# Prompts' residual rows stored to the output in the output projection, expert rows added onto them by scattering transfers

## The reference

```python
expert_id = g_sel[:, None] * EXPERTS_PER_GROUP + top_i          # two experts of each token
gate = jnp.sum(one_hot(expert_id, N_EXPERTS) * (g_w * top_p)[..., None], axis=1)
hid = silu(t @ w_gate[e]) * (t @ w_up[e]) * gate[:, e]
out = sum over e of hid @ w_down[e]
xp = xp + mp[5] * moe(modulate(xp, ...))                        # prompts: one gate row mp[5] for all tokens
xs = xs + ms[5] * moe(modulate(xs, ...))                        # samples: a gate row per token
```

## Time and profile before

| | us |
|---|---|
| median of 3 runs | 837.73 (836.27 to 840.06) |
| profiled execution, its own time | 836.97 |
| span of the profile | 835.2 |
| PE busy | 750.3 (90%) |
| DVE busy | 413.1 (49%) |
| ACT busy | 205.8 (25%) |
| POOL busy | 168.5 (20%) |

### The profile page before, as it was taken

The page is one execution under the profiler, slowest core; times in us unless marked ns, Lnnn a source line. Parts: engine busy times, 40 slices in busy tenths (PEclk is TensorE's granted clock), DMA queues, the critical chain, the costliest instruction groups (busy, mean ns, idle before and its releaser), DMA issues.

```text
span 835.2 us, 11189 instructions
## 1 busy us (share of the span) xinstructions
PE 750.3 (90%) x4235; PEld 463.8 (56%) x4235; DVE 413.1 (49%) x925; ACT 205.8 (25%) x417; POOL 168.5 (20%) x192
## 2 busy tenths in 40 slices
PE   4999989999989978999999899887999999998760
PEld 2444454588756545887886354554555555554330
DVE  4124499998798988101133123683443333333326
ACT  4012333223476664002002011122111111111100
POOL 2030030320000000443202002353223333233010
PEclk9999999999999998999999979896999999999995
DMA  8951041533236343233022902147999999999928
GB/s 350 402 179 63 2 131 39 202 114 106 101 144 260 112 189 119 110 133 127 20 101 111 407 20 101 53 177 269 412 429 423 425 424 426 423 424 422 413 124 308
DMA packets 25903, 183.65 MB, mean 220 GB/s; under 512 B 6460, under 2 KB 6884, under 8 KB 14456
## 3 DMA queue, kind: packets, MB, share of 16 engines
q1 hardware_dynamic: 15800, 161.06, 47.7%
q0 software_dynamic: 9456, 19.72, 7.1%
q10 hardware_dynamic: 592, 2.13, 0.6%
HBM read 178.59 MB, written 14.12 MB: 231 GB/s over the span
## 4 chain that ended last, share of the span: by engine, by line
PE 76%; DMA 11%; DVE 5%; ACT 4%; issue 2%; SPq 1%; POOL 1%; DVEq 0%; POOLq 0%; ACTq 0%
PE psum L735 24%; PE psum L1229 12%; PE psum L704 9%; PE psum L1243 6%; DMA arena<-in_experts 5%; PE psum L668 3%; PE psum L1130 3%; DMA arena<-in_b_router 2%; PE psum L614 2%; PE psum L1222 2%; DMA ring<-in_stream 2%; ACT arena L1588 2%; DVE arena L2576 1%; PE psum L1089 1%; PE psum L923 1%
## 5 line engine op out<-in xcount | busy, mean ns | idle before, releaser
L735 PE MATMUL psum<-hT,ring 128*128 128x260 f32 x640 | 145.8, 389 | 8.1 <-DMA ring<-in_stream 8.1
L735 PEld LDWEIGHTS psum<-hT,ring 128*128 128x128 f32 x640 | 122.5, 193 | 30.7 <-DMA ring<-in_stream 9.0
L1588 ACT ACTIVATE arena<-psum 128x512 f32<-128x512 f32 (+10 forms) x130 | 69.3, 563 | 242.6 <-PE psum L735 79.9
L704 PE MATMUL psum<-ring,hT 128*128 128x512 f32 (+1 forms) x256 | 98.0, 537 | 3.4 <-DVE arena L2298 3.4
L704 PEld LDWEIGHTS psum<-ring,hT 128*128 128x128 f32 x256 | 49.0, 197 | 50.8 <-issue 37.6
L1229 PE MATMUL psum<-ring,arena 128*64 128x256 f32 x608 | 70.5, 385 | 3.6 <-DMA ring<-in_experts 3.6
L1243 PE MATMUL psum<-arena 128*64 128x512 f32 x280 | 67.8, 604 | 3.3 <-issue 2.0
L1527 POOL DMA_INDIRECT expert_rows<-arena,router x35 | 35.4, 1010 | 154.7 <-DVE arena L2536 154.7
L1229 PEld LDWEIGHTS psum<-ring,arena 128*64 128x64 f32 x608 | 43.8, 139 | 34.2 <-issue 8.9
L735 PE MATMUL psum<-arena,ring 128*128 128x260 f32 x256 | 58.6, 392 | 0.0
L2535 DVE SCALAR_TENSOR_TENSOR arena<-psum,router,arena 128x512 f32<-128x512 f32 x35 | 26.3, 751 | 64.4 <-PE psum L1243 64.4
(11 more groups left out here) (381 smaller groups left out, 953.9 us busy)
## 6 DMA issues: line engine op xcount, KB each, us to landing
ring<-in_stream SPq DMA_DIRECT2D x21, 2048.0 KB, 8.5
ring<-in_experts SPq DMA_DIRECT2D x16, 2048.0 KB
arena<-in_experts SPq DMA_DIRECT2D x32, 1024.0 KB
arena<-in_experts SPq DMA_DIRECT2D x11, 2048.0 KB
hT<-in_experts SPq DMA_DIRECT2D x5, 2048.0 KB
ring<-expert_rows SPq DMA_DIRECT2D x8, 512.0 KB, 6.9
ring<-in_stream SPq DMA_DIRECT2D x2, 1280.0 KB, 5.6
arena<-in_x_prompt SPq DMA_DIRECT2D x4, 512.0 KB, 5.3
```

What stands on the lines that cost most here:

```text
L704: mm = pe.matmul(psum[:, b, 0:width], hT[:, k, t * P:(t + 1) * P], w[:, k, :], start=(k == 0), stop=(k == KD - 1))
L735: mm = pe.matmul(psum[:, b0 + s, 0:HALF], w[:, k, f * P:(f + 1) * P], rhs[:, k, s * HALF:(s + 1) * HALF], start=(first and k == 0), stop=( ...
L1588: ins = act.activation(out, in_, func, scale=scale)
```

## The change

- ACT stores each prompt tile of `x2` to `y_p` right behind that tile's `t2_store` (four transfers of 512 KB), counted by `sums_begun`.
- POOL stores zeros to the first 8 rows of `expert_rows`, which become the samples' sums (`zeros_stored`). The zeros come from `zero_rows`, which DVE sets beforehand. ACT waits for this store before it writes `gate_table`, which shares the space.
- `scatter` becomes two transfers per block, both with `compute_op=ALU.add`: one adds onto `y_p` by `token_tab` (bound: the prompts' rows), one onto the samples' sums by `dest_tab` (bound: 16 half rows). Each skips the other's tokens.
- A token's two picks go to the same row now, so the scatters must not overlap: `scatter(b)` waits first until both transfers of block b-1 have landed. Block 0 waits for `sums_begun` and `zeros_stored`.
- `y_stored` counts 32 per block instead of 16, and so do the waits on it.
- `dest_tab` is made in `is_sample` from `token_tab`; `sent_to` makes only `token_tab`.
- At the end SP reads the samples' sums back (32 KB), DVE multiplies them by the gate and adds them to `x2`, and SP stores `y_s`. The ten reads of picks, the ten additions on DVE and the four stores of `y_p` there are gone.
- The overflow blocks are changed likewise, with a wait behind each pair of transfers.

```diff
@@ sync
-                lone_wait(sp, over_stored, i * 32 + 32, over_passed)
+                lone_wait(sp, over_stored, i * 64 + 64, over_passed)
...
-            by_token = picks.rearrange("(c t h) n -> c t (h n)", c=2, h=2)
             for i in range(2):
-                sp.wait_ge(y_stored[i], 16 * ((N_MAIN + 1 - i) // 2))
-            for _, n, t in LAST_ORDER:
-                for c in range(2):
-                    sp.dma_start(picked[c][t][0:n], by_token[c, t * P:t * P + n, :]).then_inc(picked_in[t], 16)
-            for i, (_, n, t) in enumerate(LAST_ORDER):
-                sp.wait_ge(y_ready, i + 1)
-                dst = io["y_p"][t * P:(t + 1) * P, :] if t < NT else io["y_s"]
-                sp.dma_start(dst, x2[0:n, t, :]).then_inc(y_outs, 16)
-            sp.wait_ge(y_outs, 16 * T5)
+                sp.wait_ge(y_stored[i], 32 * ((N_MAIN + 1 - i) // 2))
+            sp.dma_start(sample_sums, io["expert_rows"][0:NS, :]).then_inc(sample_sums_in, 16)
+            sp.wait_ge(y_s_ready, 1)
+            sp.dma_start(io["y_s"], x2[0:NS, NT, :]).then_inc(y_outs, 16)
+            sp.wait_ge(y_outs, 16)
@@ gpsimd
             second_rstd(0)
+            pool.dma_start(io["expert_rows"][0:NS, :].rearrange("r (q n) -> (r q) n", q=4), zero_rows)\
+                .then_inc(zeros_stored, 16)
             second_rstd(1)
...
             def scatter(b):
                 label = BLOCKS[b][1]
-                pool.indirect_dma_start(picks, bass.IndirectOffsetOnAxis(dest_tab[:, label:label + 1], 0),
-                                        y_rows[:, b % 2, :], None, bounds_check=4 * TOK - 1, oob_is_err=False)\
-                    .then_inc(y_stored[b % 2], 16)
+                if b == 0:
+                    pool.wait_ge(sums_begun, 16 * NT)
+                    pool.wait_ge(zeros_stored, 16)
+                else:
+                    pool.wait_ge(y_stored[1 - b % 2], 32 * ((b - 1) // 2 + 1))
+                for sums, tab, rows in ((sums_p, token_tab, 2 * SEQ), (sums_s, dest_tab, 2 * NS)):
+                    pool.indirect_dma_start(sums, bass.IndirectOffsetOnAxis(tab[:, label:label + 1], 0),
+                                            y_rows[:, b % 2, :], None, bounds_check=rows - 1, oob_is_err=False,
+                                            compute_op=ALU.add).then_inc(y_stored[b % 2], 16)
@@ scalar
                 act.dma_start(io["t2_rows"][t * P:t * P + n, :], t2[i % 2][0:n, :]).then_inc(t2_stored[i % 2], 16)
+                if t < NT:
+                    act.dma_start(io["y_p"][t * P:(t + 1) * P, :], x2[:, t, :]).then_inc(sums_begun, 16)
...
             x_out(0, xT_out)
+            act.wait_ge(zeros_stored, 16)
             evac("gate_sums", ...)
@@ vector
+            lane.mark(dve.memset(zero_rows, 0.0))
...
-            banks.drained(sent_to(token_tab[:, 0:N_MAIN], dest_tab[:, 0:N_MAIN], psum[:, 4, 0:N_MAIN], sent), "tables")
+            sent_to(token_tab[:, 0:N_MAIN], psum[:, 4, 0:N_MAIN], sent).then_inc(tables_ready, 1)
+            dve.wait_ge(tables_ready, 1)
+            banks.drained(dve.tensor_copy(sent, token_tab[:, 0:N_MAIN]), "tables")
...
             def is_sample(tokens, n):
-                lane.then(dve.tensor_copy(tokens, token_tab[:, o]))
+                lane.mark(dve.tensor_scalar(prompt_skip[:, 0:n], tokens, 2.0 * SEQ, SKIP, ALU.is_lt, ALU.mult))
                 lane.then(dve.scalar_tensor_tensor(sample_gate[:, o], tokens, 2.0 * SEQ, gate_tab[:, o], ALU.is_ge, ALU.mult))
+                lane.mark(dve.scalar_tensor_tensor(dest_tab[:, o], tokens, 2.0 * SEQ, prompt_skip[:, 0:n],
+                                                   ALU.subtract, ALU.add))
...
                     if b >= 3:
-                        dve.wait_ge(y_stored[1 - p], 16 * ((b - 1) // 2))
+                        dve.wait_ge(y_stored[1 - p], 32 * ((b - 1) // 2))
...
-            for _, rows, t in LAST_ORDER:
-                dve.wait_ge(picked_in[t], 32)
-                for c in range(2):
-                    x, a = x2[0:rows, t, :], picked[c][t][0:rows]
-                    if t == NT:
-                        lane.then(dve.tensor_tensor(a, a, gate2_s[0:NS], ALU.mult))
-                    ins = dve.tensor_tensor(x, x, a, ALU.add)
-                    lane.then(ins) if c == 0 else ins.then_inc(y_ready, 1)
+            dve.wait_ge(sample_sums_in, 16)
+            lane.then(dve.tensor_tensor(sample_sums, sample_sums, gate2_s[0:NS], ALU.mult))
+            dve.tensor_tensor(x2[0:NS, NT, :], x2[0:NS, NT, :], sample_sums, ALU.add).then_inc(y_s_ready, 1)
```

More of the change, by code:

```diff
@@ L414, in decoder_step @@
         sent = at(6656, N_MAIN)
+        prompt_skip = at(6656 + 192, N_MAIN)
         r = sb("router", [P, 630])
@@ L469, in decoder_step @@
         over_sent = at(6656 + 2 * SB, N_OVER)
-        picked = [[ring[:, 1 + c, t * D:(t + 1) * D] for t in range(NT)]
-                  + [hT.rearrange("p k n -> p (k n)")[:, c * D:(c + 1) * D]] for c in range(2)]
+        sample_sums = x_rows[0:NS, 0:2, :].rearrange("p b n -> p (b n)")
+        zero_rows = at(32768, 256)[0:4 * NS]
         bank_full = [sem(f"bank_full{b}") for b in range(8)]
@@ L533, in decoder_step @@
         over_scaled, over_gated = sem("over_scaled"), sem("over_gated")
-        picked_in = [sem(f"picked_in{t}") for t in range(T5)]
-        y_ready = sem("y_ready")
+        sums_begun, zeros_stored, sample_sums_in, y_s_ready = (
+            sem(n) for n in ("sums_begun", "zeros_stored", "sample_sums_in", "y_s_ready"))
         ws_masked = sem("ws_masked")
@@ L551, in decoder_step @@
         last_use = {}
-        LAST_ORDER = [("S", NS, NT), (0, P, 0), (1, P, 1), (2, P, 2), (3, P, 3)]
         ROUTE = [(P, 0), (NS, NT), (P, 1), (P, 2), (P, 3)]
@@ L557, in decoder_step @@
         half_rows = io["t2_rows"].rearrange("r (h n) -> (r h) n", h=2)
-        picks = io["expert_rows"].rearrange("r (h n) -> (r h) n", h=2)[0:4 * TOK, :]
+        sums_p = io["y_p"].rearrange("r (h n) -> (r h) n", h=2)
+        sums_s = io["expert_rows"].rearrange("r (h n) -> (r h) n", h=2)[0:2 * NS, :]
         def lone_wait(engine, semaphore, value, passed):
@@ L1547, in pool_pair @@
                 for n in range(2):
-                    pool.wait_ge(y_stored[n], 16 * ((N_MAIN + 1 - n) // 2))
+                    pool.wait_ge(y_stored[n], 32 * ((N_MAIN + 1 - n) // 2))
                 for j in range(2):
@@ L1567, in pool_pair @@
                     lone_wait(pool, over_y_out, i * 2 + j + 1, over_passed)
[L1568 to L1571, removed]
+                    for sums, tab, rows in ((sums_p, next_token, 2 * SEQ), (sums_s, next_dest, 2 * NS)):
+                        pool.indirect_dma_start(sums, bass.IndirectOffsetOnAxis(tab[:, j:j + 1], 0),
+                                                y_rows[:, j, :], None, bounds_check=rows - 1, oob_is_err=False,
+                                                compute_op=ALU.add).then_inc(over_stored, 16)
+                    lone_wait(pool, over_stored, i * 64 + 32 * j + 32, over_passed)
                 pool.sem_inc(over_go, 1)
@@ L2430, in _, with sent_to @@
                 psum[0:NE, 2, 0:P].rearrange("p (h n) -> p h n", h=2), 2, 2)), "picks")
-            def sent_to(token, dest, V, tmp):
+            def sent_to(token, V, tmp):
                 lane.then(dve.tensor_scalar(tmp, V, C("second_at"), -2.0 * TOK, ALU.is_ge, ALU.mult))
-                ins = dve.scalar_tensor_tensor(token, V, C("half_at"), tmp, ALU.add, ALU.add)
-                ins.then_inc(tables_ready, 1) if tmp is sent else lane.mark(ins)
-                return dve.tensor_scalar(dest, V, C("half_at"), None, ALU.add)
+                return dve.scalar_tensor_tensor(token, V, C("half_at"), tmp, ALU.add, ALU.add)
             banks.wait_full(dve, "tables")
-            banks.drained(sent_to(token_tab[:, 0:N_MAIN], dest_tab[:, 0:N_MAIN], psum[:, 4, 0:N_MAIN], sent), "tables")
+            sent_to(token_tab[:, 0:N_MAIN], psum[:, 4, 0:N_MAIN], sent).then_inc(tables_ready, 1)
+            dve.wait_ge(tables_ready, 1)
+            banks.drained(dve.tensor_copy(sent, token_tab[:, 0:N_MAIN]), "tables")
             banks.wait_drained(dve, "tables")
@@ L2453, in is_sample @@
             def is_sample(tokens, n):
-                if n == N_MAIN:
-                    dve.wait_ge(tables_ready, 1)
                 o = slice(0, N_MAIN) if n == N_MAIN else slice(N_MAIN, N_BLOCKS)
-                lane.then(dve.tensor_copy(tokens, token_tab[:, o]))
+                lane.mark(dve.tensor_scalar(prompt_skip[:, 0:n], tokens, 2.0 * SEQ, SKIP, ALU.is_lt, ALU.mult))
                 lane.then(dve.scalar_tensor_tensor(sample_gate[:, o], tokens, 2.0 * SEQ, gate_tab[:, o], ALU.is_ge, ALU.mult))
+                lane.mark(dve.scalar_tensor_tensor(dest_tab[:, o], tokens, 2.0 * SEQ, prompt_skip[:, 0:n],
+                                                   ALU.subtract, ALU.add))
                 lane.then(dve.tensor_tensor(gate_tab[:, o], gate_tab[:, o], sample_gate[:, o], ALU.subtract))
```

(3 more changed lines are left out.)

## The result

| | before | after |
|---|---|---|
| median of runs | 838.89 us | 927.18 us (922.60 to 928.72) |
| span of the profiled execution | 835.2 | 926.3 |

The ratio is 1.1035, 95% interval 1.0968 to 1.1103: the change makes the kernel 10.4% slower. The forecast was slower, 892 us, range 834 to 955.

A forecast was written before the change was run, and what follows sets the result against it. PE paced the expert blocks until 748, then weight transfers, with the DMA engines full. Span 835.2 + 65.6 for awaited landings - 10.8 at the end = 890.0, plus 1.8 gives 892 us; range 834 to 955.

The forecast's parts named there:

- The end: From the last scatter's issue to the end of the span: 22.4 us become 11.6, so 10.8 us go.
- The moved stores: Four stores of prompt rows, moved behind the stores of normed rows, cost 0; 2.5 us if not hidden.
- The period: Expert blocks: time from one block's first add to the next one's, 9.0 us taken, 8.0 to 10.6 as bounds.
- ten packets per engine instead of five: A block's pair of adds beside weights: ten packets per engine take 4.8 to 8.4 us.
- rival 3: Expert blocks: adds go out in smaller packets, 18 per pair, period 11.0 us, time 946 us; chance 0.17.
- my own case: The main forecast: period from 8.0 to 10.6 us, time 865 to 935 us, 892 likeliest; chance 0.57.
- The mix: Expert blocks: weights stand in the way 7.8 us of each period, 9.2 to 12.8 us full, 4.4 free, giving 8.7 to 10.6.
- The start of a landing: On full engines, 3.6 us before an add's first packets go.
- The landing on free engines: Period on free engines: 0.8 for POOL's start, 1.32 for the second issue, 2.28 to land, together 4.4 us.
- The engines' load: DMA engines: one more read of each added row, 0 to 10.0 us, hidden in the wait.
- rival 1: Expert blocks: the wait is hidden and the adds are free, only the end shrinks, 826 us; chance 0.15.
- rival 2: Expert blocks: the wait is hidden, the second read is paid with 10.0 us, time 839 us; chance 0.11.

The follow-up runs named there:

- the two experiments with one half of the change each: On the kernel before: each scatter waits until the previous one has landed, 875.71 us; scatters add, with no wait between them, 857.93 us.
- experiment 3: The changed kernel with both transfers of a block plain instead of adding, all waits kept: 892.60 us.
- experiments 9 to 11: Expert weights in 4 KB pieces on three kernels: the one before, 837.37 us; with adding scatters, 854.33 us; with scatters waiting for the previous one, 841.07 us.
- experiment 5: The changed kernel (as `after_4k`) with expert weights loaded in pieces of 4 KB per partition: 899.83 us.
- add_only_4k: The kernel before with adding scatters, no wait between them, and expert weights in 4 KB pieces: 854.33 us.
- before_4k: The kernel before with expert weights in 4 KB pieces and nothing else changed: 837.37 us.
- after_no_weights: The changed kernel loading no expert weights beyond the first six experts, which later blocks use again: 820.31 us.
- wait_only_4k: The kernel before with plain scatters that each wait for the one before, and expert weights in 4 KB pieces: 841.07 us.

## Why the prediction was right

**The direction and its mechanism** were right. The waits, the chain and the two experiments with one half of the change each show that the landing of one block's adds became the stage's period.

**The end** was right: 22.4 us should become 11.6; it is 926.3 - 914.63 = 11.7. **The moved stores** cost nothing, as forecast: the first scatter is issued at 593.16 instead of 594.37. **The last blocks**, 6 x 6.2 + 3.8 = 41 forecast, took 39.0.

**The period** was under-sized: 9.0 forecast, 10.46 measured, which is 39 us over 27 periods; the last blocks and the earlier start gave 3 back, and the span came out 36 us over the forecast 890.0. The step that failed is "ten packets per engine instead of five". An adding transfer has nine packets per engine, the skipping one too (2 x 144 packets over 16 engines), which fits one for each of eight rows and one to signal the end. That was rival 3, which I gave 0.17; its period of 11.0 and 946 us are nearer than mine. With ten packets and short issues (experiment 3) the time is 892.60 and the mean period 8.9, what the sum with ten had given. That the measured time still lies inside my own case, 865 to 935, is in part luck: its upper end was ten packets at 0.84 us, 8.4 us, and what came was eighteen at some 0.43, 7.7 us.

**The mix** of full and free engines was right in kind and rough in size. The first two periods, with the engines full, are 14.8 and 14.2 us, more than the 9.2 to 12.8 of my sum and the 13.0 of rival 3; those on free engines are 5.4 to 5.8. With these two ends my formula would give some 11.5, an estimate, where 10.46 was measured. Only two of the 27 single periods lie within the 8 to 10.6 us that I had named as a sign of being right.

**The start of a landing** was under-sized as well: 3.6 us from one scatter; 3.7 to 4.9 in the first four blocks here, with the engines full. Part of it is the longer issue (1.57 instead of 1.0 us). **The landing on free engines**, 4.4 forecast, is 5.4 to 5.7 with the longer issues (1.58 + 0.30 before the second, then 2.9).

**The engines' load** for the second read was set at 10 us and hidden under the wait. It is some 14 us (experiments 9 to 11). By an estimate it would also be the floor under every repair: the end gains 10.8, so even with the whole chain of landings hidden this change would not pay, which no run here shows by itself. With that load rival 1 could not have come about, and rival 2 would have ended at some 843 instead of 839.

**What stays open:** why nothing of POOL's queue moves for 4 to 5 us after the issue of an add beside weights, where it is 2.1 on free engines. It isn't the size of the weight packets (experiment 5). A kernel with fewer weights in flight was not tried.

No version with all its weights loaded beat the kernel before.

## What to carry to other kernels

A transfer that nobody waits for has no visible price; before putting a wait behind it, look up in the queues how long it lands beside the traffic of that stage (7.8 us here against 2.3 on free engines), and compare that with the period of the loop. Count packets, not bytes: a queue of small transfers beside a saturated stream of large ones advanced here by one packet for each large one, so many small packets, even of skipped rows, are what costs, and cutting the stream into 4 KB pieces bought part of that back for nothing (the loss from one wait fell from 4.1% to 0.7%). And moving work out of a kernel's end into a stage in which the DMA engines are full pays only if the engine time of its bytes, reads of an addition included, is less than the time won at the end.

## What the runs showed of the hardware

- A scatter that adds takes 1.55 to 1.63 us to issue on POOL, a plain one 1.0, and goes out as 144 packets for 128 rows where the plain one has 80.
- An add costs the engines 217 engine-us more than the plain writes of the same 2080 rows of 2 KB: about 0.10 us of one engine for each row. In `add_only_4k` the packet of an added row takes 0.18 us, where in `before_4k` a packet with two plain rows takes 0.16.
- Loading the same weights in packets of 4 KB instead of 8 and 16 KB made no difference (ratio 1.0015), and PE's pace stayed 6.2 us until it waited for weights.
- With full engines the first packets of an add go 3.7 to 4.9 us after its issue beside large weight packets (first four blocks of the changed kernel) and 4.7 to 4.8 beside small ones (first seven of `after_4k`), and 2.1 us after it on free engines (`after_no_weights`). For a plain scatter it is 3.4 (the kernel before, at 786.00) to 4.2 (first seven blocks of `wait_only_4k`) with full engines and 1.6 on free ones.
